# One hybrid layer on one core: the first block's memory, attention, state space and expert order rewritten

## The chip, the cores and the metric

The kernel runs on one core of one Trainium2 chip. A core has TensorE (PE: matmuls; its weight loads are shown as PEld), VectorE (DVE), ScalarE (ACT), GpSimd (POOL) and SyncE (SP), each with an instruction queue of its own that is worked off in order; they meet at semaphores. 16 DMA engines move data between HBM and the on-chip memory. The metric is device time of one launch in microseconds; the median of three runs is compared.

## The reference

Everything is fp32, one sequence of 256 rows of 1024. Two blocks follow each other; the change is in the first.

```
h = rms_norm(x, attn_norm_w)
z, xbc, dt, q, k, v, g_ssd, g_att = split(h @ w_in)            # 1024 x 7440
y_ssd = state_space(z, xbc, dt) @ w_ssd_out   # conv of 4, 16 heads of 64, 2 groups, chunks of 128; times silu(z); group norm
y_att = causal_attention(rope(q), rope(k), v) @ w_attn_out     # 16 heads of 64
x = x + (sigmoid(g_ssd) * y_ssd + sigmoid(g_att) * y_att) @ w_out
h = rms_norm(x, moe_norm_w)
x = x + moe(h)                  # 4 groups of 8 experts: one group, two experts a row; 1024 -> 256 -> 1024
x = x + sigmoid(rms_norm(x, ple_norm_w) @ w_ple_gate) * (p @ w_ple)
x = rms_norm(x, final_norm_w)
```

The second block (a long convolution beside a latent attention) takes this result. Its code changes only in a function's name and in where two vectors of norm weights are loaded and multiplied.

## The kernel before

**Products.** A fp32 product is made of three matmuls in a faster format (`mul3`): high part by high part, low by high and high by low. Weights come as tiles of 1 MB (four chunks of 128 rows by 512 columns) into four raw buffers; ACT makes the high part `WH` and DVE the low part `WL`, into three split slots. `weights(n)` splits every tile whose slot is free once tiles before n have been consumed; it stands at fixed places of the ACT and DVE queues. `gemm` multiplies two halves of 128 rows by a tile pair, 8 chunks of 6 matmuls. `transposed` turns a 256-row operand on TensorE into PSUM, and `high` and `low` split it on ACT and DVE.

**PSUM.** The 8 banks are handed out in turn by `ring.take(name, drainer)`, which makes TensorE wait until the drainer of the bank's last holder is done with it. `ring.of` narrows the set of banks.

**Order.** First norm, transposes; a transpose "colp" that turns row vectors (convolution weights and others) into columns; channel groups cx 0 to 2 (`channels`) with the convolution on ACT and DVE (`convolved`, L1759); q and k with rope on DVE (L1781 to L1789); v 0 and v 1; the state space's products cb and pv; transposes of q and k; attention head by head, with `fill` giving TensorE chunks of the z products between heads; the state space with chunks of the g products between its steps; the transposed attention output `oT`, the projections wao, wso, wo; the router `lg`; ranks; experts. Gates and z are drained by ACT with Sigmoid or Silu (`drain`, L1203).

**Experts.** Each row is copied into a slot of its experts (32 slots an expert). `gather` makes the slot inputs by matmuls with one-hot matrices; its stationary operands XNh and XNl are high and low parts of the normalized rows, written by ACT (L1374) and DVE (L2001). For q in 0 to 7, four experts are worked at a time: gate, up, down. Their 96 weight tiles, and one ("wpl") for a side product, are used unsplit, each in one of `NHELD` held buffers, which are carved out of memory that the first block no longer needs. Side products for rows that overflowed their slots' count are made near the end.

**SP's queue.** SP issues all weight DMAs in the order of use: `fetch(k)` (L2524) for dense tiles, which waits until the raw buffer's tile before was split, then `fetch_held(t)` (L2552) for expert tiles. A held buffer's first tile waits for the last reader of that memory, a later one for the last matmul of the tile before. `held_to` and `last_five` keep some buffers out of the rotation and say where the last five tiles go:

```python
held_to = {0: 0, 1: 0, 5: 0, 6: 0, 7: 0, 14: 56, 15: 56, 8: 68, 10: 85, 11: 85}
last_five = {92: 14, 93: 15, 94: 12, 95: 13, 96: 19}
...
for k in range(NRAW, dense_again):
    fetch(k)
for t in range(len(moe_tiles)):
    fetch_held(t)
```

## Time and profile before

| | |
|---|---|
| median of 3 runs | 888.27 us (887.16 to 888.43) |
| profiled execution | 888.41 us, span 886.6 us |
| mean granted TensorE clock | 0.942 of full speed |
| TensorE busy | 773.9 us, 87% |
| DVE, ACT, POOL busy | 472.9, 334.9, 17.8 us |
| DMA moved | 190.24 MB, 215 GB/s over the span |

The span is the time from the first to the last recorded instruction of one profiled execution; the metric has 1.8 us more around it. In the rows below times are microseconds from the span's start. A timeline's line is one instruction or several alike that follow each other (x16); "[5.30 <-DMA ...]" is the idle time of the engine before it and what ended it. In `pb<-HTh,WH` the operand that streams is named first and the stationary one second. Matmul durations overlap: the distance from one start to the next is what a matmul costs.

### The profile page before, as it was taken

The numbers are of one execution on the slowest core, as the hardware profiler recorded it, in microseconds if no ns is written. First come the engines' busy times: TensorE is split into PE (matmuls) and PEld (weight loads), VectorE is DVE, ScalarE is ACT, GpSimd is POOL, SyncE is SP. The second block draws the span as 40 slices with busy tenths as digits, with TensorE's granted clock in tenths as the row PEclk, the third lists the DMA queues.
The fourth block names the chain that finished last, engine by engine and source line by source line (L and its number), as shares of the span: only waits on it lengthen the run. The fifth ranks groups of instructions, "written<-read, shape, count | busy, mean of one in ns | idle before, by whom it ended". The sixth has DMA issues, their size and how long they took to land.

```text
span 886.6 us, 11023 instructions
## 1 busy us (share of the span) xinstructions
PE 773.9 (87%) x4618; PEld 578.0 (65%) x4618; DVE 472.9 (53%) x812; ACT 334.9 (38%) x487; POOL 17.8 (2%) x14
## 2 busy tenths in 40 slices
PE   2999798897998989797776988778999999999888
PEld 2988676676776877554442444335899965578676
DVE  4668946554666654722312411216777786754653
ACT  6454344543553422521100110105765534257512
POOL 0000000000000000000000000000010003000000
PEclk9999899898998999899888988988999999999989
DMA  8555541211442377989999999992455562433201
GB/s 268 196 185 194 190 136 55 95 48 52 142 139 95 97 273 320 422 318 407 420 422 421 421 421 420 421 390 75 152 191 173 166 237 95 143 110 124 99 1 48
DMA packets 62558, 190.24 MB, mean 215 GB/s; under 512 B 7405, under 2 KB 11751, under 8 KB 50024
## 3 DMA queue, kind: packets, MB, share of 16 engines
q1 hardware_dynamic: 60730, 184.70, 56.1%
q10 hardware_dynamic: 1774, 4.79, 1.7%
q8 instruction: 38, 0.62, 0.3%
q14 instruction: 16, 0.13, 0.0%
HBM read 188.42 MB, written 1.05 MB: 214 GB/s over the span
## 4 chain that ended last, share of the span: by engine, by line
PE 62%; DMA 16%; DVE 12%; ACT 7%; issue 2%; SPq 1%; POOL 0%; ACTq 0%; DVEq 0%
PE pb L498 59%; DMA raw<-in_w_exp_up 5%; DMA WHo<-in_w_exp_up 4%; DVE WL L1646 4%; ACT WH L1172 4%; DMA WLo<-in_w_exp_up 3%; PE pb L507 3%; DMA XN<-in_w_exp_up 3%; DMA arena<-in_final_norm_w 1%; DVE cv_ L1759 1%; ACT arena L1203 1%; SPq L2524 1%; SPq L2567 1%; DVE arenao L2001 0%; ACT arenao L1196 0%
## 5 line engine op out<-in xcount | busy, mean ns | idle before, releaser
L1646 DVE TENSOR_TENSOR WL<-raw,WH 128x2048 fp32r<-128x2048 f32 (+5 forms) x80 | 173.4, 2178 | 116.5 <-ACT WH L1172 116.5
L498 PE MATMUL pb<-WH,HTh 128*128 128x512 f32 (+2 forms) x416 | 171.6, 413 | 22.9 <-DVE HTl L1675 7.4
L1172 ACT ACTIVATE WH<-raw 128x2048 fp32r<-128x2048 f32 (+5 forms) x80 | 144.9, 1822 | 117.1 <-PE pb L498 113.3
L498 PE MATMUL pb<-WH,HTl 128*128 128x512 f32 (+2 forms) x416 | 163.4, 393 | 0.0
L498 PE MATMUL pb<-WL,HTh 128*128 128x512 f32 (+2 forms) x416 | 163.4, 393 | 0.0
L498 PEld LDWEIGHTS pb<-WH,HTh 128*128 128x128 f32 x416 | 80.5, 193 | 47.6 <-issue 7.3
L498 PEld LDWEIGHTS pb<-WL,HTh 128*128 128x128 f32 x416 | 80.2, 193 | 16.5
L498 PEld LDWEIGHTS pb<-WH,HTl 128*128 128x128 f32 x416 | 80.6, 194 | 14.8 <-issue 1.0
L498 PE MATMUL pb<-raw,arena 128*32 128x256 f32 x368 | 59.5, 507 | 18.8 <-DMA raw<-in_w_exp_up 9.1
L498 PE MATMUL pb<-arena 128*32 128x256 f32 (+6 forms) x284 | 71.3, 433 | 4.3 <-DMA arena<-in_w_exp_up 1.9
L2160 DVE TENSOR_TENSOR rt_<-rt_,pb 128x256 f32<-128x256 f32 x8 | 3.4, 422 | 109.1 <-ACT rt_ L1421 109.1
L498 PE MATMUL pb<-HTh,WH 128*128 128x256 f32 (+1 forms) x184 | 53.4, 290 | 0.0
L498 PE MATMUL pb<-HTh,WL 128*128 128x256 f32 (+1 forms) x184 | 53.0, 288 | 0.0
L498 PE MATMUL pb<-HTl,WH 128*128 128x256 f32 (+1 forms) x184 | 53.0, 288 | 0.0
L498 PEld LDWEIGHTS pb<-raw,arena 128*32 128x32 f32 x368 | 25.6, 143 | 40.6 <-issue 12.4
L498 PEld LDWEIGHTS pb<-arena 128*32 128x32 f32 (+4 forms) x284 | 34.3, 159 | 22.8 <-issue 9.3
L1421 ACT ACTIVATE rt_<-pb 128x256 f32<-128x256 f32 x8 | 3.1, 383 | 115.6 <-PE pb L498 115.6
L498 PE MATMUL pb<-WHo,arena 128*32 128x256 f32 (+1 forms) x160 | 38.3, 478 | 7.6 <-DMA WHo<-in_w_exp_up 5.6
L498 PE MATMUL pb<-XN,arena 128*128 128x64 f32 (+2 forms) x160 | 41.5, 414 | 2.8 <-DMA XN<-in_w_exp_up 1.8
L498 PE MATMUL pb<-WH,arenao 128*128 128x512 f32 x128 | 39.8, 392 | 0.0
L507 PE MATMUL pb<-c,arena 128*128 128x128 f32 (+2 forms) x202 | 29.2, 279 | 11.2 <-DMA arena<-in_final_norm_w 5.3
L507 PEld LDWEIGHTS pb<-c,arena 128*128 128x128 f32 (+2 forms) x202 | 24.5, 157 | 18.0 <-DMA arena<-in_final_norm_w 5.7
(357 smaller groups left out, 1308.6 us busy)
## 6 DMA issues: line engine op xcount, KB each, us to landing
raw<-in_w_in SPq DMA_DIRECT2D x46, 1024.0 KB, 5.1
raw<-in_w_exp_up SPq DMA_DIRECT2D x13, 1024.0 KB, 21.6
raw<-in_w_exp_gate SPq DMA_DIRECT2D x10, 1024.0 KB, 23.7
WLo<-in_w_exp_down SPq DMA_DIRECT2D x10, 1024.0 KB, 19.6
raw<-in_w_out SPq DMA_DIRECT2D x8, 1024.0 KB, 5.4
WHo<-in_w_exp_down SPq DMA_DIRECT2D x8, 1024.0 KB, 19.4
raw<-in_w_attn_out SPq DMA_DIRECT2D x6, 1024.0 KB, 5.5
arena<-in_w_exp_up SPq DMA_DIRECT2D x5, 1024.0 KB, 11.8
```

The lines of the kernel that those rows point to most:

```text
L498: return e.matmul(o, l, r, start=start, stop=stop, skip_group_check=True)
L507: return e.transpose(o, i, ident[0:k, 0:k])
L1172: e.activation(h_, r_, ACT.Copy).then_inc(hi.sem, hi.mark(k))
L1203: e.activation(dst[:, t, :], pb((name, t))[:, 0:n], f, scale=scale).then_inc(ac.sem, ac.mark((name, t)))
L1421: e.activation(HG[q % 2], pb(("gu", q))[:, 0:256], ACT.Silu).then_inc(ac.sem, ac.mark(("su", q)))
L1646: e.tensor_tensor(l_, r_, h_.bitcast(F32), ALU.subtract).then_inc(lo.sem, lo.mark(k))
L1759: e.scalar_tensor_tensor(out=cv[:, s:L], in0=u[:, 0:L - s], scalar=cw[:, 3 - s, g:g + 1], in1=cv[:, s:L], op0=ALU.mult, op1=ALU.add).then_inc(
L2160: e.tensor_tensor(HG[q % 2], HG[q % 2], pb(("gu", q))[:, 256:512], ALU.mult).then_inc(ve.sem, ve.mark(("gu", q)))
L2524: e.dma_start(dst[:, :, col:col + v.shape[2]], v).then_inc(d.sem, d.mark(k, by=16))
L2567: e.dma_start(dst, src).then_inc(d_rows.sem, d_rows.mark("in", by=16))
```

## The change

- *Start:* DVE scales both halves of the first norm (before, ACT scaled one), the first tile is split ahead of it, and "colp" is turned after the first channel group.
- *Rope and v:* the tile that falls due is split before the rope except for the last one; v 0 takes the banks of the xs transposes; q's and k's transposes stand between v 0 and v 1.
- *Attention:* two heads a step in two banks, 11 steps with two chunks of z or g each; mask and maximum in one DVE operation; eight score buffers instead of four.
- *z and g:* drained by plain copies; Silu of z's left half and the Sigmoids of g run later on ACT from memory.
- *State space:* by groups of 8 heads, the product of a group one step behind its decay rows; the attention output's transposes and splits stand between the steps, into buffers of their own (OT).
- *Transposes by halves:* mT inside wso 1 and wo 0, nm inside wo 1 and the router (`halves_T`). Rows of w_out and the routers are taken in "(c p)" order.
- *Gather:* XNh and XNl are contiguous rows in HT's memory, and the gather's stationary operand has a step of 8 elements.
- *Experts:* 19 held buffers instead of 20, in another order, x no longer among them. SP issues expert tiles 0 to 5 between dense tiles and 6 and 7 right behind them on conditions of that stage; two routers' DMAs stand behind dense tile 7.

```diff
-NHELD = 20
+NHELD = 19
...
+        OT = tuple(arena_r[:, o:o + 2048].rearrange("p (c l) -> p c l", c=8) for o in (6656, 0))
...
+        XNh, XNl = (x.rearrange("p c l -> p (c l)").rearrange("p (t d) -> p t d", t=2) for x in HT)
...
+        XG = [x.rearrange("p (c e) -> p c e", c=8) for x in (X.rearrange("p t d -> p (t d)"), arena[:, 6144:8192])]
...
+        for key, w, rows_ in (("wao", wao, "(p c)"), ("wso", wso, "(p c)"), ("wo", wo, "(c p)")):
...
+        held = [part(16896), part(12800), part(2048), part(4096), XN.rearrange("p t d -> p (t d)"), part(10752), part(8704),
+                part(14848), *last_raw, *[x[:, s, :] for s in emptied for x in (WHf, WLf)], part(0)]
...
+        held_to = {0: 0, 1: 0, 5: 0, 7: 0, 16: 56, 17: 56, 6: 68, 3: 80, 12: 85, 13: 85, 4: 76}
+        last_five = {92: 16, 93: 17, 94: 14, 95: 15, 96: 4}
...
             rows_T("n1")
+            channels(("cx", 0), [("xbc", g) for g in range(4)], 512, "n1", [ve] * 4)
             d_rows.wait_ge(e, "in")
-            turn(ring.take("colp", ve)[:, 0:122], rows[0:122, :]).then_inc(mm.sem, mm.mark("colp"))
-            channels(("cx", 0), [("xbc", g) for g in range(4)], 512, "n1", [ve] * 4)
+            turn(ring.take("colp", ve)[:, 0:114], rows[0:114, :]).then_inc(mm.sem, mm.mark("colp"))
             channels(("cx", 1), [("xbc", g) for g in range(4, 8)], 512, "n1", [ve] * 4)
             channels(("cx", 2), [("xbc", 8), ("xbc", 9), "dtT"], 272, "n1", [ve, ve, ac])
...
+            gemm(("v", 0), ("v", 0), HT, "n1", (ve, ac), [where[("xs", t, 0)] for t in range(2)])
...
+            gemm(("v", 1), ("v", 1), HT, "n1", (ve, ac))
...
+            def scores(j):
+                o = [ring.take(("s", h), ve) for h in (2 * j, 2 * j + 1)]
                 for n in ("qT", "kT"):
                     ve.wait_ge(e, (n, 4))
                     ac.wait_ge(e, (n, 6))
-                mul(o[:, 0:128], QT[of:of + 64, j, 0:128], KT[of:of + 64, j, 0:128])
-                mul(o[:, 128:384], QT[of:of + 64, j, 128:256], KT[of:of + 64, j, 0:256]).then_inc(
-                    mm.sem, mm.mark(("s", h)))
+                for t in range(2):
+                    w = 128 * (t + 1)
+                    for i, of in enumerate((0, 64)):
+                        ins = mul(o[i][:, 128 * t:128 * t + w], QT[of:of + 64, j, t * 128:t * 128 + 128],
+                                  KT[of:of + 64, j, 0:w])
+                        if t:
+                            ins.then_inc(mm.sem, mm.mark(("s", 2 * j + i)))
...
+            for j in range(11):
+                if j < 8:
+                    scores(j)
+                fill(1)
+                if 2 <= j <= 9:
+                    weights_T(2 * j - 4)
+                    weights_T(2 * j - 3)
+                fill(1)
+                if j >= 3:
+                    values(2 * j - 6)
+                    values(2 * j - 5)
...
+            def attended_T(js):
+                for j in js:
+                    o = ring.take(("oT", "T", j), ve)
+                    ve.wait_ge(e, ("o", 1, 0), ("o", 1, 1))
+                    for c in (j, j + 1):
+                        for t in range(2):
+                            o_ = (c - j) * 256 + t * 128
+                            ins = turn(o[:, o_:o_ + 128], O[:, t, slice(c, c + 127 * 8 + 1, 8)])
+                    ins.then_inc(mm.sem, mm.mark(("oT", "T", j)))
+
+            def states(t, g):
+                o = ring.take(("y", t, g), ve)
+                ve.wait_ge(e, ("km", t, g))
+                for h in range(8 * g, 8 * g + 8):
+                    ins = mul(o[:, (h - 8 * g) * 64:(h - 8 * g) * 64 + 64], LM[:, h, :], XD[:, t, h * 64:h * 64 + 64])
+                ins.then_inc(mm.sem, mm.mark(("y", t, g)))
+                if t == 1:
+                    o = ring.take(("yi", g), ve)
+                    ve.wait_ge(e, ("pv", 0))
+                    ac.wait_ge(e, ("pv", 1))
+                    mul(o[:, :], XBC[g * 64:g * 64 + 64, 9, 128:256], PV[g * 64:g * 64 + 64, :]).then_inc(
+                        mm.sem, mm.mark(("yi", g)))
...
+            def halves_T(name, src, half, ready):
+                ve.wait_ge(e, ready)
+                for j in (4 * half, 4 * half + 2):
+                    o = ring.take((name, "T", j), ve)
+                    for c in (j, j + 1):
+                        for t in range(2):
+                            o_ = (c - j) * 256 + t * 128
+                            ins = turn(o[:, o_:o_ + 128], src[:, t, c * 128:c * 128 + 128])
+                    ins.then_inc(mm.sem, mm.mark((name, "T", j)))
...
+            for k in range(5):
+                if k < 4:
+                    decay_rows(k // 2, 8 * (k % 2))
...
+                    decay_rows(k // 2, 8 * (k % 2) + 4)
+                    fill(2)
+                if k in (1, 2):
+                    attended_T((4 * k - 4, 4 * k - 2))
+                if k:
+                    states((k - 1) // 2, (k - 1) % 2)
+                    fill(2)
...
-            gemm(("wao", 0), ("wao", 0), HT, "oT", (ve, ve))
+            gemm(("wao", 0), ("wao", 0), OT, "oT", (ve, ve))
             ve.wait_ge(e, "yn")
             transposed("yT", lambda t: XN[:, t, :], 8)
-            gemm(("wao", 1), ("wao", 1), HT, "oT", (ve, ve))
-            for i in range(2):
-                gemm(("wso", i), ("wso", i), YT, "yT", (ve, ve))
-            ve.wait_ge(e, ("mg", 1))
-            transposed("mT", lambda t: MG[:, t, :], 8)
...
+            def gemm_around(key, lhs, ready, at, between):
+                o = [ring.take((key, t), ve) for t in range(2)]
+                for c in range(8):
+                    gemm_chunk(key, key, c, o, lhs, ready)
+                    if c == at:
+                        between()
+
+            gemm_around(("wso", 1), HT, "yT", 4, lambda: halves_T("mT", MG, 0, ("mg", 0)))
+            gemm_around(("wo", 0), OT, "mT", 2, lambda: halves_T("mT", MG, 1, ("mg", 1)))
+            gemm_around(("wo", 1), OT, "mT", 4, lambda: halves_T("nm", X, 0, ("x mix", 0)))
+
...
+            for half in range(2):
+                for c in range(4 * half, 4 * half + 4):
+                    ve.wait_ge(e, ("nm", c))
+                    ins = mul3(o[0:36, 0:256], tuple(x[:, c, :] for x in WR), tuple(x[:, c, :] for x in HT), c == 0,
+                               c == 7)
+                if half == 0:
+                    halves_T("nm", X, 1, ("x mix", 1))
...
-                            ins = mul(o[:, (c % 2) * 256:(c % 2) * 256 + 256], x[:, t, c, :],
+                            ins = mul(o[:, (c % 2) * 256:(c % 2) * 256 + 256], x[:, t, slice(c, c + 127 * 8 + 1, 8)],
...
+                if name == ("z", 0):
+                    drain(name, Z[:, :, 0:512], ACT.Copy)
+                elif name == ("z", 1):
+                    ac.wait_ge(e, (("z", 0), 1))
+                    e.activation(Z[:, :, 0:512], Z[:, :, 0:512], ACT.Silu).then_inc(ac.sem, ac.mark("z left"))
+                    drain(name, Z[:, :, 512:1024], ACT.Silu)
...
+                    mm.wait_ge(e, ("s", 15))
+                    drain(name, (GS, GA)[i // 2][:, :, 512 * (i % 2):512 * (i % 2) + 512], ACT.Copy)
...
+            weights(None, 1)
...
+            for i in (2, 3, 0, 1):
+                gv = (GS, GA)[i // 2][:, :, 512 * (i % 2):512 * (i % 2) + 512]
+                ac.wait_ge(e, (("g", i), 1))
+                e.activation(gv, gv, ACT.Sigmoid).then_inc(ac.sem, ac.mark(("gate 1", i)))
...
+                for t in range(2):
+                    e.tensor_scalar(XN[:, t, :], src[:, t, :], norm_of[n][:, t:t + 1], None, ALU.mult).then_inc(
+                        ve.sem, ve.mark(("xn", n)))
...
+            mm.wait_ge(e, "colp")
+            e.tensor_copy(colp, pb("colp")[:, 0:114]).then_inc(ve.sem, ve.mark("colp"))
...
+                weights(used((n, i)) - 1)
...
+                for t, cut in enumerate((slice(0, 128), slice(128, 384))):
+                    ins = e.tensor_tensor_reduce(S1[s][:, cut], pb(("s", h))[:, cut], C["matt"][:, cut], -0.125, 3.0e38,
+                                                 ALU.add, ALU.min, nmx[:, s, t:t + 1])
+                ins.then_inc(ve.sem, ve.mark(("s", h), ("mx", h)))
...
-                e.scalar_tensor_tensor(out=XNl[:, t, :, :], in0=Xc[:, t, :, :], scalar=rnm[:, t:t + 1],
-                                       in1=XNh[:, t, :, :].bitcast(F32), op0=ALU.mult, op1=ALU.subtract).then_inc(
+                e.scalar_tensor_tensor(out=XNl[:, t, :], in0=X[:, t, :], scalar=rnm[:, t:t + 1],
+                                       in1=XNh[:, t, :].bitcast(F32), op0=ALU.mult, op1=ALU.subtract).then_inc(
...
+                elif i == 2:
+                    mm.wait_ge(e, ("yi", 1), ("oT", "T", 6))
+                elif i == 3:
+                    ve.wait_ge(e, "yn")
+                elif i == 4:
+                    mm.wait_ge(e, ("yT", "T", 6))
+                elif i == 5:
                     ve.wait_ge(e, (("wao", 1), 1))
+                elif i == 6:
+                    ve.wait_ge(e, ("mg", 1))
+                elif i == 7:
+                    mm.wait_ge(e, ("mT", "T", 6))
                 elif i in held_raw:
...
+            early = {used_before(("wso", 0), 4): (0, 1, 2), used_before(("wso", 1), 4): (3, 4),
+                     used_before(("wo", 0), 4): (5,)}
+            for k in range(8, dense_again):
+                fetch(k)
+                for t in early.get(k, ()):
+                    fetch_held(t)
+            for t in range(6, len(moe_tiles)):
                 fetch_held(t)
```

## Rows read from the trace of the kernel before

**Rows 1.** The page, busy time of the engines over the span.

```profile
PE 773.9 (87%) x4618; PEld 578.0 (65%) x4618; DVE 472.9 (53%) x812; ACT 334.9 (38%) x487; POOL 17.8 (2%) x14
```

**Rows 2.** Busy time by stretch; columns: stretch, length, engines' busy time (instructions), clock, DMA share, GB/s.

```profile
98.43:138.73 40.30, 32.65 (x164) 26.51 (x163) 26.09 (x33) 16.68 (x20) 0.00 (x0) 0.92 0.49 156
206.86:278.78 71.92, 64.69 (x341) 53.62 (x342) 44.14 (x65) 36.29 (x39) 0.00 (x0) 0.97 0.38 123
278.78:354.06 75.28, 72.24 (x320) 59.36 (x320) 39.45 (x48) 22.01 (x21) 1.01 (x1) 0.96 0.55 202
393.43:587.10 193.67, 157.06 (x1343) 79.14 (x1336) 46.94 (x113) 20.63 (x38) 0.00 (x0) 0.89 1.01 415
```

**Rows 3.** SP's timeline; columns: start, length, queue, line, operation, target<-source, count.

```profile
321.48 2.66 SPq L2552 DMA_DIRECT2D arena<-in_w_exp_gate  x2
...
371.08 0.33 SPq L2552 DMA_DIRECT2D X<-in_w_exp_up  x1
382.26 3.78 SPq L2552 DMA_DIRECT2D raw<-in_w_exp_down  x3
393.43 0.33 SPq L2552 DMA_DIRECT2D arena<-in_w_exp_down  x1
...
572.58 0.33 SPq L2552 DMA_DIRECT2D X<-in_w_exp_down  x1
```

**Rows 4.** TensorE's timeline, stalls before the first expert; in brackets idle time before and releaser.

```profile
19.34 0.47 PE L507 MATMUL pb<-c,arena 122*128 122x122 f32 x1 [5.30 <-DMA arena<-in_final_norm_w]
...
106.35 0.77 PE L498 MATMUL pb<-WH,HTh 128*128 128x512 f32 x1 [5.33 <-DVE rt_ L1784]
...
135.11 2.84 PE L507 MATMUL pb<-c,arena 128*128 128x128 f32 x24 [1.55 <-DVE arena L1685]
...
204.25 2.82 PE L498 MATMUL pb<-arena,rt_ 128*128 128x64 f32 x12 [5.76 <-DVE rt_ L1685]
...
278.78 0.77 PE L498 MATMUL pb<-WH,HTh 128*128 128x512 f32 x1 [3.88 <-DVE HTl L1675]
...
329.76 2.06 PE L507 MATMUL pb<-c,arena 128*128 128x128 f32 x16 [2.84 <-DVE arena L1974]
...
371.09 6.37 PE L498 MATMUL pb<-cv_o,arenao 128*128 128x256 f32 x32 [4.36 <-DVE arenao L2001]
```

**Rows 5.** ScalarE's timeline, a high part near the start.

```profile
33.64 1.79 ACT L1172 ACTIVATE WH<-raw 128x1904 fp32r<-128x1904 f32 x1 [3.28 <-PE pb L498]
```

**Rows 6.** VectorE's timeline, the operations used as prices.

```profile
37.52 1.90 DVE L1759 SCALAR_TENSOR_TENSOR cv_<-pb,small,cv_ 128x255 f32<-128x255 f32 x4
...
100.63 2.29 DVE L1646 TENSOR_TENSOR WL<-raw,WH 128x2048 fp32r<-128x2048 f32 x1 [0.95 <-ACT WH L1172]
...
268.60 1.22 DVE L1915 TENSOR_TENSOR arena<-arena,cv_ 128x1024 f32<-128x1024 f32 x1
...
365.89 2.05 DVE L2001 SCALAR_TENSOR_TENSOR arenao<-X,small,arenao 128x1024 fp32r<-128x1024 f32 x1
```

**Rows 7.** TensorE's timeline, the product cb and one head's step.

```profile
130.06 0.72 PE L498 MATMUL pb<-arena 64*128 64x128 f32 x8
...
176.00 0.92 PE L498 MATMUL pb<-arena 64*128 64x128 f32 x4
176.85 0.50 PE L498 MATMUL pb<-WH,HTh 128*128 128x512 f32 x1
...
178.34 0.49 PE L507 MATMUL pb<-c,arena 128*128 128x128 f32 x3
...
179.38 0.48 PE L498 MATMUL pb<-arena 64*128 64x128 f32 x2
```

**Rows 8.** TensorE's timeline, transposes whose stationary operand has a step of 8.

```profile
272.86 2.05 PE L507 MATMUL pb<-c,arena 128*128 128x128 f32 x16
```

**Rows 9.** TensorE's timeline, the side products and the last "down".

```profile
585.22 7.03 PE L498 MATMUL pb<-XN,arena 128*128 128x512 f32 x16
596.72 1.06 PE L498 MATMUL pb<-WLo,rt_ 128*32 128x512 f32 x1 [4.48 <-issue]
```

More of the change, by code:

```diff
@@ new lines, in scalar @@
+            for j in range(11):
+                if j < 8:
+                    exps1(2 * j)
+                    exps1(2 * j + 1)
+                fill(1)
+                if 2 <= j <= 9:
+                    h = 2 * j - 3
+                    if h >= 4:
+                        mm.wait_ge(e, ("pv1", h - 4))
+                    drain_t(("p", h), P1[:, h % 4, 0:384])
+                fill(1)
+            for k in range(5):
+                if k < 4:
+                    for h0 in (8 * (k % 2), 8 * (k % 2) + 4):
+                        ve.wait_ge(e, ("lm", k // 2, h0))
+                        e.activation(LM[:, h0:h0 + 4, :], LM[:, h0:h0 + 4, :], ACT.Exp).then_inc(
+                            ac.sem, ac.mark(("lm", k // 2, h0)))
+                        fill(2)
+                if k in (1, 2):
+                    high("oT", OT, 4 * k, after=("pv1", 15), first=4 * k - 4)
+                if k:
@@ new lines, in vector, with decay_rows @@
+                fill(1)
+                if j in (6, 10):
+                    divided(2 * j - 5)
+            def decay_rows(t, h0):
+                mm.wait_ge(e, ("lm", t, h0))
+                if t:
+                    mm.wait_ge(e, ("y", 0, h0 // 8))
+                for h in range(h0, h0 + 4):
+                    ins = e.scalar_tensor_tensor(
+                        out=LM[:, h, :], in0=pb(("lm", t, h0))[:, (h - h0) * 128:(h - h0) * 128 + 128],
+                        scalar=Ac[:, t, h:h + 1], in1=C["mneg"], op0=ALU.subtract, op1=ALU.add)
+                ins.then_inc(ve.sem, ve.mark(("lm", t, h0)))
@@ new lines, in vector @@
+            mm.wait_ge(e, ("p", 15))
+            for k in range(5):
+                if k < 4:
+                    for h0 in (8 * (k % 2), 8 * (k % 2) + 4):
+                        decay_rows(k // 2, h0)
+                        fill(2)
+                    skipped(k // 2, k % 2)
+                if k in (1, 2):
+                    low("oT", OT, 4 * k, first=4 * k - 4)
+                if k:
+                    states((k - 1) // 2, (k - 1) % 2)
+                if k < 4:
+                    t, g = k // 2, k % 2
@@ L1986, in residual @@
                         ve.sem, ve.mark((name, t), event))
-            for i in range(2):
-                residual(("wo", i), i, ("x mix", i))
-                weights(used(("wo", i)))
+            residual(("wo", 0), 0, ("x mix", 0))
+            weights(used(("wo", 0)))
+            low("nm", HT, 4, mnc)
+            residual(("wo", 1), 1, ("x mix", 1))
             ve.wait_ge(e, ("x mix", 1))
```

384 lines of the change are left out of this document (144 added, 240 removed).

## The prediction

> **What bounds the kernel now.** I read the page first, then busy time by stage, then SP's queue, then TensorE's timeline for its stalls and the other engines' beside them. The page shows TensorE busy 87% of the span [rows 1]: a gain must come out of its idle stretches or its work, wherever TensorE sets the pace. The windows show where it does not. From 393.4 to 587.1 the DMA share is 1.01 at 415 GB/s while TensorE works 157 of 193.7 us [rows 2]; 415 GB/s is 2.5 us for each tile of 1 MB. So the expert phase is bound by the transfer, with 36.6 us of slack on TensorE. Everything before it, and everything behind it, goes by TensorE.
>
> What links the two is SP's queue [rows 3]. Expert tiles start at 321.48, and after 382.26 SP issues three and then nothing until 393.43, when the first "down" releases a buffer; from there the queue runs full. The transfer-bound stretch therefore begins when TensorE reaches the first "down". A microsecond saved before it moves the whole stretch one microsecond. The early issue itself fetches tiles that are due anyway before that point: at 393.43 all the held tiles are in, and no buffer is free for another. Counting tiles by the order of releases, 23 are fetched or under way at the first "down" in either version and 74 remain, with 19 buffers as with 20. I cost the early issue and the smaller ring at nothing. The cover is the stretch in which SP waits (382.26 to 393.43); without it each tile by which the queue starts richer would be worth 2.5 us.
>
> The sum is made against the profiled execution, 888.4 us (span 886.6), 0.1 above the median shown, 888.27. About 0.2% (1.8 us) is what a measurement of this kernel can tell from no change.
>
> **A, the start.** TensorE waits 5.30 us for the DMA of the row vectors before the "colp" transpose at 19.34 [rows 4]. That transpose moves behind the first channel group, so the group starts 4.9 earlier. But banks are taken round-robin: "colp" no longer takes the bank after the first transposes, so the fourth bank of the second channel group is now the one that xbc 0 holds, which DVE frees only at the end of `convolved(0)`. In front of that stand ACT's two high parts and first tap (1.8 for a high part [rows 5]) and DVE's two low parts and three scalar-tensor steps (2.3 each, and 0.5 each from four in 1.90 [rows 6]), in order: from about 26.8, when ACT gets to them by my count, to about 34.6. TensorE, done with group 0 near 27.6, idles about 7, starts group 1 at 34.6 against 32.2 before, and loses about 2 more to a lowered clock, as after the 5.33 stall at 106.35, where a matmul took 0.77 against 0.50 at full clock [rows 4, 7]. A 0.8 stall behind it goes away. Cost +1.9; bounds −4.9 (no bank wait) to +2.7.
>
> **B, rope to scores** (98.43, where k1 ends, to 138.73, where the first scores start: 40.3 us [rows 2]). Before, v0 waits 5.33 for rope's last read of its bank at 106.35 [rows 4]. After, rope's tile is split before the rope and v0 takes the xs banks, so what is late is the split behind the WL at 100.63 [rows 6]: v0 starts near 101.7, 3.3 after k1. Then 11 for v0, 32 transposes at 0.12 (24 took 2.84 at 135.11 [rows 4]) with 1 us of waits, 4.5 together, 11 for v1, and 5.5 until scores (a high and low part, a copy of v, a copy of cb), against 8.7 before. 35.3: −5.0. Bounds: TensorE's whole idle time of the stage, 7.65 [rows 2], gone; or only the one at v0 shortened, −1.
>
> **C, attention** (138.73 to 206.86, 68.1 us, with 16 z chunks). A head's step took 3.38: scores 0.85, a chunk 1.49 (178.34 less 176.85), and 1.04 for three transposes and the six matmuls of the values, of which I give the transposes 0.33 and the values 0.71 [rows 7]. Two heads at rows 0 to 63 and 64 to 127, into two banks, may run side by side: the eight 64-row matmuls of cb alternate halves and took 0.72 in all, less than the 0.92 of one head's four [rows 7]. I take 0.95 for a pair (bounds 0.85 to 1.7). A pair's step is then 0.95 + 2 × 1.4 + 0.66 + 1.42 + 0.16 of seams = 5.99 against 6.76. Eight of these and six chunks more at 1.4 are 56.3, 0.4 for the first exponentials, 1.3 for banks that wait behind the Silu of z: 58.0. So −10.1, though six g chunks (8.3 us) are already in it. The stall of 5.76 at 204.25 [rows 4], TensorE waiting for the last heads' copies with nothing to fill, is filled by them. The mask and maximum in one DVE pass replace four DVE operations; nothing like it is in the trace (from one 0.56 add to the add and two reductions), and DVE is off the path here, so 0. Bounds −14 to −4 (pairs not concurrent: 8 × 0.75 more).
>
> **D, state space** (206.86 to 278.78, 71.9 us [rows 2]). Six g chunks fewer: −8.3. TensorE idles 7.23 there [rows 2]: 3.88 at the end, waiting for the transposed attention's low part at 278.78 [rows 4], and 3.35 inside, before chunks whose bank ACT drains with a table to load. The drains are plain copies now and the transposes and splits are done inside: −7.2. New: the first decay bank is held by the division of heads 8 to 15 (+1.9), the last group's product (+0.7), and wao's bank behind the last g drain (+1.2). −11.7. Bounds −15.5 to −6.
>
> **E, output projections** (278.78 to 354.06, 75.3 us [rows 2]). wao 0 took 13.5 instead of 11 because its clock had fallen (the stage's first matmul takes 0.77 and not 0.50 [rows 4, 7]); the 2.84 wait for mT at 329.76 [rows 4] and its transposes are put between chunks by halves. New: four sigmoids on ACT after g stand before the state space's norm, near 12.4 us after g 3 with table load, squares and scaling, of which 0.3 shows behind wao 0's 11. 66 for six projections, 0.3, 1.75 for yT, 2.7 for halves: 71.0, −4.3. Bounds −5 to −2.
>
> **F, routing to the first "down"** (354.06 to 393.43). Half of nm's transposes move into wo 1: −1.9. Two low parts of the gather on DVE, 2.05 each through a strided view [rows 6], become contiguous; 1.22 is the row for as many contiguous elements [rows 6]: −1.7. ACT's highs shrink too; DVE waits for the first of them alone, and I add nothing. −3.6; bounds −6 (the gather's 32 matmuls at 371.09 took 6.37 after a stall of 4.36, at the lower clock [rows 4]) to 0. **A rule that speaks against this.** The contiguous halves are now read with a step of 8 elements, 32 bytes, as the gather's stationary operand. The Trainium skill, SBUF — State Buffer, section Door 1: The DMA port swizzle, says that a 16-byte line must be hit twice to hide its latency, and that fp32 can be strided by up to 4 elements for free. By it DVE gains here, as the two rows show, and the gather's weight loads lose; it gives no price, and the sum by it is rival 3's. The trace has 16 transposes with such a stationary operand in 2.05 [rows 8], 0.13 each, against 0.12 of the contiguous ones at 135.11 [rows 4]: by these the sum stays, and I add nothing.
>
> **H, the tail.** Buffers for the last tiles change. Before, the last expert tile is issued at 572.58 [rows 3] and waits for nothing on TensorE's side. After, tile 95 takes the buffer of the overflow weights, so SP can issue it only when the 16 side products at 585.22 are done, 592.3 [rows 9]. It and the last tile behind it land some 5 and 7.7 us later, at 600.0, against the last "down" at 596.72 [rows 9]: +3.3, bounds 0 to +5.
>
> Sum: +1.9 − 5.0 − 10.1 − 11.7 − 4.3 − 3.6 + 3.3 = −29.5; small new waits that I can't place, +1.5. −28.0: **860.4 us**. Its own range is 851 to 868.
>
> **Rivals.**
> 1. *In-order queues eat half of C and D* (0.17). DVE is busy 44.1 of D's 71.9 [rows 2]; with the transposed attention's low parts (2.5) and without the splits of six g chunks (3.4) it must fit 43 into 60; the queue is in order, so an early decay step waits behind a fill's split. For it: stalls like 204.25 and 278.78 were all on DVE [rows 4]. Against: 0.72 busy fits. Half of 21.8 lost gives 871 (868 to 880).
> 2. *Less stands in the way than I charge* (0.13). No bank wait at the start (−6.8 against A), the gather at full clock (−2.4), no extra waits (−1.5): 849.7; with the tail also free 846. If instead the queue did start richer by eight tiles, 20 us less: 840; SP's idle stretch [rows 3] speaks against it.
> 3. *The strided gather* (slower, 0.06). 128 matmuls read the strided halves: 48 before the first "down", the other 80 inside the phase with 36.6 us of slack [rows 2]. To undo 28 it must cost (28 + 36.6)/128 = 0.50 us a matmul more, from there on the time is above 888, at 0.6 about 901. The strided transposes' 0.01 [rows 8] speaks against it.
> 4. *The gains don't carry* (0.04): something else, such as the last held tile's arrival, sets the first "down", and the phase starts at its old time: 888 ± 1.8. SP's rows show the last of the first tiles issued at 371.08 and the first release only at 382; after the change they are issued earlier still.
>
> **How the numbers follow.** My forecast, 0.60: 851 to 868. With the shares above, 846 leaves out about 0.06 of rival 2, and 877 about 0.03 of rival 1 and all of rivals 3 and 4: the range 846 to 877 leaves out a little under 0.2. Faster 0.90, same 0.04, slower 0.06.
>
> **What would show it.** After: TensorE's first channel group near 14.6, then an idle 7 ended by DVE's convolution (A); no stall before v0 over 4 (B); pairs of scores near 0.95 and a pair's step near 6 (C); the first output projection near 254, at full clock (D, E); the first "down" near 361, and from it tiles every 2.5 us until the last but two; SP's tile behind the side product, and the last "down" 3 later than the side products' end gives (H); the last 285 us as long as before. Wrong if the first "down" moves and the end doesn't, if scores of a pair take 1.7, or if the gather's matmuls are slower than 0.3.

## The result, and the profile after

The changed kernel takes 874.6 us (median of 4 runs, 871.98 to 877.03) against 888.35 before in the same comparison: 0.9845 of the time (95% interval 0.9814 to 0.9876), 13.8 us less. A second set of 5 runs gave 873.84 and again 0.9845 (0.9826 to 0.9865). The forecast was 28.0 less, 860.4. The sign was right and 874.6 lies in the wide range (846 to 877), but it is outside the forecast's own range (851 to 868), and the gain is 13.8 of the 28.0 that were forecast, a little under half. The profiled execution took 874.9 us, span 873.1, 13.5 less than before.

The page of the changed kernel, busy times (answers to [rows 1]):

```profile
PE 771.7 (88%) x4618; PEld 580.5 (66%) x4618; DVE 459.9 (53%) x813; ACT 326.1 (37%) x483; POOL 17.8 (2%) x14
```

TensorE is busy 2 us less than before, DVE and ACT 13 and 9 us less. Of the 13.5 us that the span lost, 11.3 are idle time of TensorE, as the forecast wanted it; there is less of it than forecast.

Busy time by stretch of the changed kernel, columns as in [rows 2]: rope and v, attention, state space, output projections, routing to the first "down", expert phase. The fifth ends where the first "down" frees a buffer and SP issues the next tile (372.22 below); TensorE starts that "down" at 368.02.

```profile
101.05:135.33 34.28, 30.88 (x164) 25.08 (x163) 24.97 (x33) 17.00 (x20) 0.00 (x0) 1.00 0.54 181
135.33:201.28 65.95, 58.77 (x340) 47.45 (x340) 28.81 (x87) 32.93 (x84) 0.00 (x0) 0.92 0.27 86
201.28:261.30 60.02, 57.06 (x305) 47.46 (x305) 39.47 (x62) 22.43 (x27) 0.00 (x0) 0.97 0.33 103
261.30:331.62 70.32, 70.24 (x329) 58.29 (x329) 41.75 (x49) 31.87 (x35) 1.01 (x1) 1.00 0.78 306
331.62:372.22 40.60, 33.90 (x275) 23.61 (x277) 18.49 (x71) 11.44 (x23) 0.70 (x1) 0.87 0.64 253
372.22:560.34 188.12, 153.28 (x1288) 81.82 (x1284) 45.27 (x107) 20.27 (x37) 0.00 (x0) 0.91 1.00 406
```

These stretches end at the same events as the terms B to F of the sum, and the last one where the 94th of the 97 tiles lands. (That landing, 560.34 here and 579.61 before, is read from the trace's DMA records; SP issued it at 543.15 below.) So term stands against measurement:

| term | before | after | change | forecast |
|---|---|---|---|---|
| A, start to the end of k1 | 98.43 | 101.05 | +2.6 | +1.9 |
| B, to the first scores | 40.30 | 34.28 | −6.0 | −5.0 |
| C, attention | 68.13 | 65.95 | −2.2 | −10.1 |
| D, state space | 71.92 | 60.02 | −11.9 | −11.7 |
| E, output projections | 75.28 | 70.32 | −5.0 | −4.3 |
| F, to the first "down" | 39.37 | 40.60 | +1.2 | −3.6 |
| expert phase, to the 94th tile | 186.18 | 188.12 | +1.9 | 0 |
| the rest (tail H, second block) | 307.00 | 312.76 | +5.8 | +3.3 |
| small waits, not placed | | | | +1.5 |
| sum | | | −13.5 | −28.0 |

A, B, D and E are right within 1.0 each. C is 7.9 off, F 4.8, the two last stretches 4.4. How far one execution can be trusted shows in a second trace of the changed kernel, from the second set of runs: C 67.09, F 41.75 and the expert phase 186.64 instead of 65.95, 40.60 and 188.12, A 0.6 longer, B, D and E within 0.03.

TensorE's timeline of the changed kernel, its stalls and one pair of scores (answers to [rows 4] and [rows 7]):

```profile
14.97 0.35 PE L497 MATMUL pb<-HTh,WH 128*128 128x256 f32 x1 [0.72 <-DVE HTl L1727]
...
34.34 0.58 PE L497 MATMUL pb<-HTh,WH 128*128 128x256 f32 x1 [7.52 <-DVE cv_ L1806]
...
104.29 0.47 PE L497 MATMUL pb<-WH,HTh 128*128 128x512 f32 x1 [0.65 <-ACT arena L1234]
...
135.33 0.93 PE L497 MATMUL pb<-arena 64*128 64x128 f32 x8 [2.75 <-DVE cv_ L1900]
...
152.68 0.87 PE L506 MATMUL pb<-c,arena 128*128 128x128 f32 x6 [1.16 <-DVE rt_ L1733]
...
156.15 0.93 PE L497 MATMUL pb<-arena 64*128 64x128 f32 x8
...
183.79 0.77 PE L497 MATMUL pb<-WH,HTh 128*128 128x512 f32 x1 [4.41 <-ACT arena L1230]
...
201.28 1.62 PE L497 MATMUL pb<-c,small 128*128 128x128 f32 x8 [1.62 <-DVE arena L1931]
```

The first channel group starts at 14.97 and the 7.52 us idle behind it, ended by DVE's convolution, is what term A foresaw (14.6 and about 7). The 5.33 before v0 is 0.65. The eight score matmuls of two heads take 0.85 (156.15 to 157.00), as much as four of one head did before, and less than the 0.95 that was taken. But there are four stalls inside the attention and at its end (2.75, 1.16, 4.41, 1.62), for which the sum has 1.7 in C and 1.9 in D; the first of them (at 135.33) lies in B's last 5.5, as forecast, and behind it the granted clock falls to the lower level in this execution.

ScalarE's timeline of the changed kernel ahead of the 4.41:

```profile
180.37 1.28 ACT L1246 ACT_TABLE_LOAD   x1
181.66 1.06 ACT L1246 ACTIVATE arena<-arena 128x1024 f32<-128x1024 f32 x1
182.62 1.07 ACT L1230 ACTIVATE arena<-pb 128x512 f32<-128x512 f32 x2
```

ACT loads a table, takes the Silu of z's left half out of memory, and only then drains z's second half with Silu; 183.69 is when the second of these drains ends, and 0.1 later TensorE goes on. The chunks that fill the steps have two banks of their own, and g's first chunk needs them. (Of z only the left half is drained by a plain copy.) The exponentials ahead of the table load start late as well. ACT's first of them, and DVE's timeline before it:

```profile
178.12 0.40 ACT L1356 ACTIVATE arena<-arena,small 128x128 f32<-128x128 f32 x1 [4.74 <-DVE small L1920]
```

```profile
173.03 2.29 DVE L1693 TENSOR_TENSOR WL<-raw,WH 128x2048 fp32r<-128x2048 f32 x1 [3.18 <-ACT WH L1202]
...
177.45 0.28 DVE L1920 CUSTOM_DVE_ANT_0 arena<-pb,c 128x128 f32<-128x128 f32 x1
```

TensorE had finished this pair's scores at 174.32. DVE worked off a low part (2.29), a copy and the division of heads 0 to 7 first and began their mask and maximum (L1920) at 177.45; ACT stood idle for 4.74 until then.

### The profile page after: what moved, and what is told of

The parts are those of the page before. It is cut to its first block, busy times and chain, and to the rows that moved or that the text cites. A ratio compares the mean times of both kernels' runs of the same rounds, so it can differ in the third digit from the quotient of the medians.

```text
span 873.1 us, 11016 instructions
## 1 busy us (share of the span) xinstructions
PE 771.7 (88%) x4618; PEld 580.5 (66%) x4618; DVE 459.9 (53%) x813; ACT 326.1 (37%) x483; POOL 17.8 (2%) x14
## 4 chain that ended last, share of the span: by engine, by line
PE 60%; DMA 17%; DVE 12%; ACT 8%; issue 2%; POOL 0%; SPq 0%; ACTq 0%; DVEq 0%
PE pb L497 57%; DMA raw<-in_w_exp_up 7%; DVE WL L1693 5%; DMA WHo<-in_w_exp_up 5%; ACT WH L1202 4%; PE pb L506 3%; DMA WLo<-in_w_exp_up 3%; DMA raw<-in_w_in 1%; DMA XN<-in_w_exp_down 1%; DVE cv_ L1806 1%; ACT arena L1230 1%; ACT arena L1356 1%; DVE HTl L1727 0%; ACT arena L1388 0%; POOL small L2572 0%
## 5 line engine op out<-in xcount | busy, mean ns | idle before, releaser
L497 PE MATMUL pb<-WH,HTh 128*128 128x512 f32 (+2 forms) x384 | 158.4, 413 | 16.5 <-ACT arena L1230 5.4
L497 PE MATMUL pb<-WH,HTl 128*128 128x512 f32 (+2 forms) x384 | 150.1, 391 | 0.0
L497 PE MATMUL pb<-WL,HTh 128*128 128x512 f32 (+2 forms) x384 | 150.0, 391 | 0.0
L497 PE MATMUL pb<-arena 128*32 128x256 f32 (+6 forms) x252 | 59.0, 444 | 3.2 <-DVE cv_ L1900 2.8
L497 PE MATMUL pb<-WH,arenao 128*128 128x512 f32 x192 | 59.9, 393 | 1.2 <-ACT arena L1230 1.2
L497 PE MATMUL pb<-raw,arena 128*32 128x256 f32 x224 | 37.4, 520 | 10.3 <-DMA raw<-in_w_exp_gate 6.2
L497 PEld LDWEIGHTS pb<-WH,arenao 128*128 128x128 f32 x192 | 35.6, 188 | 8.9 <-ACT arena L1230 1.6
L497 PEld LDWEIGHTS pb<-HTh,WH 128*128 128x128 f32 (+1 forms) x184 | 35.2, 191 | 9.2 <-DVE cv_ L1806 7.7
L497 PE MATMUL pb<-WL,arenao 128*128 128x512 f32 x96 | 37.4, 390 | 0.0
L497 PEld LDWEIGHTS pb<-HTh,WL 128*128 128x128 f32 (+1 forms) x184 | 35.3, 192 | 0.2
```

What stands on the lines that cost most here:

```text
L497: return e.matmul(o, l, r, start=start, stop=stop, skip_group_check=True)
```

## The experiments

Each run is the changed kernel with the edit shown; its ratio is to the kernel before, and the changed kernel's is 0.9845 (0.9814 to 0.9876). "Less" compares medians with the changed kernel's 874.6.

### The last tiles' buffers (H)

```diff
-        last_five = {92: 16, 93: 17, 94: 14, 95: 15, 96: 4}
+        last_five = {84: 18, 85: 15, 91: 12, 92: 16, 93: 17, 94: 14, 95: 15, 96: 4}
...
+            if t in last_five and i in ring:
+                ring.remove(i)
```

> The changed kernel, with other buffers for the last expert tiles: the fourth and third of the last five now go where a tile of the seventh quarter lay, and the side product's weights move to a buffer that no last tile needs. Theory: in the changed kernel two of the last tiles wait at SP for TensorE (issued at 564.40 and 574.16 after the tile before them at 543.15) and so the last one lands at 583.01 and the last down starts its last products at 583.06. With the buffers free earlier all are issued by about 550 and land by about 568, and the last down starts when the side products and the branch behind them are over, near 577 to 578.5: 4.5 to 6 us less, about 869 to 870. Rival: the side products and the norm weights behind them set the end anyway, less than 1.5 us.

869.72 us, 0.9787 (0.9768 to 0.9805): 4.9 less. SP's and TensorE's timelines, first the changed kernel:

```profile
332.66 26.18 SPq L2624 DMA_DIRECT2D arena<-in_w_exp_up  x2
358.88 0.43 SPq L2624 DMA_DIRECT2D arena<-in_w_exp_down  x1
...
372.22 0.33 SPq L2624 DMA_DIRECT2D raw<-in_w_exp_down  x1
...
543.15 0.43 SPq L2624 DMA_DIRECT2D WLo<-in_w_exp_down  x1
564.40 0.33 SPq L2624 DMA_DIRECT2D WHo<-in_w_exp_down  x1
574.16 0.33 SPq L2624 DMA_DIRECT2D WLo<-in_w_exp_down  x1
```

```profile
567.10 7.03 PE L497 MATMUL pb<-WLo,arena 128*128 128x512 f32 x16
575.64 0.62 PE L497 MATMUL pb<-WLo,rt_ 128*32 128x512 f32 x1 [1.51 <-issue]
...
579.23 1.92 PE L497 MATMUL pb<-WLo,rt_ 128*32 128x512 f32 x2 [2.54 <-DMA WLo<-in_w_exp_down]
583.06 1.06 PE L497 MATMUL pb<-XN,rt_ 128*32 128x512 f32 x1 [1.91 <-DMA XN<-in_w_exp_down]
```

and with the edit:

```profile
542.95 0.43 SPq L2626 DMA_DIRECT2D WLo<-in_w_exp_down  x1
543.42 0.43 SPq L2626 DMA_DIRECT2D WHo<-in_w_exp_down  x1
552.69 0.33 SPq L2626 DMA_DIRECT2D WLo<-in_w_exp_down  x1
```

```profile
567.79 7.03 PE L499 MATMUL pb<-arena 128*128 128x512 f32 x16
579.24 1.06 PE L499 MATMUL pb<-WLo,rt_ 128*32 128x512 f32 x1 [4.42 <-issue]
```

The waits at SP (564.40 for a buffer that the "up" of the last four experts reads, 574.16 for the side products, which take 567.10 to 574.1) are gone, and the last "down" starts whole at 579.24 where its last tile's products started at 583.06. The mechanism of H is shown; its size was 4.9 by the medians and not 3.3. One thing is left open: between the side products and the last "down" TensorE stands 1.51 in the changed kernel and 4.42 with the edit, as before the change [rows 9], at the same branch.

### The bank at the start (A), and whether the start carries

```diff
+            colp_bank = ring.take("colp", ve)
             channels(("cx", 0), [("xbc", g) for g in range(4)], 512, "n1", [ve] * 4)
...
-            turn(ring.take("colp", ve)[:, 0:114], rows[0:114, :])
+            turn(colp_bank[:, 0:114], rows[0:114, :])
```

> The changed kernel, with the bank of the row vectors' transpose taken ahead of the first channel group (the transpose itself stays behind it). The second group's fourth bank is then that one again and not the one that the first convolution holds. Theory: the idle 7.52 us at 34.34 goes away, and about 1.5 of lowered clock behind it; the next waits give back 0 to 2. First down 6.5 to 9 us earlier, and the whole as much: 866 to 868. Rival: the split of the next tiles and the convolutions in VectorE's queue take its place, 3 us or less gained. Second rival: the start moves by 7 but the end does not, because the expert phase is not released by TensorE's first down.

865.27 us, 0.9744 (0.9723 to 0.9766): 9.3 less, 0.7 below the range that was expected. The second group's start, and the first scores:

```profile
27.58 0.38 PE L497 MATMUL pb<-HTh,WH 128*128 128x256 f32 x1 [0.37 <-DVE small L1798]
...
126.95 0.92 PE L497 MATMUL pb<-arena 64*128 64x128 f32 x7 [2.75 <-DVE cv_ L1901]
```

The 7.52 is 0.37. First scores at 126.95 instead of 135.33, the first "down" at 360.78 instead of 368.02, the span 863.7 instead of 873.1. What is saved at the start arrives at the end, through the transfer-bound phase, as the forecast had it: an earlier TensorE frees the buffers earlier that SP's queue waits for.

### The Silu of z (C)

```diff
-                    ac.wait_ge(e, (("z", 0), 1))
-                    e.activation(Z[:, :, 0:512], Z[:, :, 0:512], ACT.Silu)...
-                    drain(name, Z[:, :, 512:1024], ACT.Silu)
+                    drain(name, Z[:, :, 512:1024], ACT.Copy)
...
+            for i in range(2):      # after the attention's steps
+                zv = Z[:, :, 512 * i:512 * i + 512]
+                e.activation(zv, zv, ACT.Silu)...
```

> The changed kernel, with the second half of z drained by a plain copy too and both Silus done between the attention and the state space. Theory: TensorE's stall of 4.41 us at 183.79 is the wait for the two fixed banks of the filling products, and 2.3 of it are the table load and the Silu of the left half that ScalarE does before it drains; it falls to about 2, and part of the 1.9 us of lowered clock behind it goes too: 2.3 to 4 us less, 870.5 to 872.5. Rival: the stall comes from VectorE, whose mask and maximum stand behind a split and hold back ScalarE's exponentials; less than 1 us gained.

869.63 us, 0.9788 (0.9748 to 0.9829): 5.0 less by the medians, where 2.3 to 4 were expected, but the interval overlaps the changed kernel's. The attention takes 62.84 in the profile. With its code unchanged it took 63.9 to 67.1 in six traces, whose stalls are the same within 0.03; what differs is the time at the lower clock behind them. So the stall itself is the measure here:

```profile
181.01 0.77 PE L497 MATMUL pb<-WH,HTh 128*128 128x512 f32 x1 [2.02 <-ACT arena L1230]
```

The stall falls from 4.41 (4.40 or 4.41 in all six traces) to 2.02, by the 2.3 that stood on ACT in front of the drain. The rest is the wait for one pair of banks, which ACT drains behind the exponentials of its step; and those start late, as shown above, because DVE's mask and maximum stand behind a low part and a division. That part is read from the trace; no run moved the work on DVE there.

### The g products out of the attention (C)

The lists of work to fill with get g behind the attention's loop instead of ahead of it, in all three queues.

> The changed kernel, with the g products kept out of the attention (the attention's steps are filled by z alone, as before the change; the state space gets all 32 chunks of g). Theory: what the six chunks of g in the attention save by covering the last heads (a stall of 5.8 before the change) they lose again, since the first of them waits 4.41 us for the two fixed banks of the filling products and runs 1.9 slower behind that: within 2 us of the changed kernel, 872.5 to 876.5. Rival: the cover is worth the full 5 to 6 us, 879 to 881.

876.29 us, 0.9866 (0.9841 to 0.9891), 1.7 more than the changed kernel and within what can't be told from it.

```profile
187.30 5.38 PE L497 MATMUL pb<-arena,rt_ 128*128 128x64 f32 x24 [6.35 <-DVE rt_ L1733]
194.30 1.01 PE L497 MATMUL pb<-c,small 128*128 128x128 f32 x3 [1.62 <-DVE arena L1929]
```

The end of the attention now stalls 6.35 with nothing to fill, as it did before the change (5.76, [rows 4]); and the stall of 4.41 is not there. Attention and state space take 127.6 us together, against 126.0 (123.6 to 127.1 in the six traces with the attention of the changed kernel). So the cover that C counted on is real, a stall of 6.35, and the bank's wait behind z took most of it back.

### The gather's operands (F)

XNh and XNl are laid out as before the change: `"p (t c j) -> p t c j"`, written through a strided view of x, read by TensorE as `x[:, t, c, :]`.

> The changed kernel, with the gather's two operands laid out as before the change: written through a strided view by ScalarE and VectorE, read by TensorE contiguously. Theory: the step of 8 elements costs each gather matmul about 0.05 us at the lower clock and 0.10 at the full one; 32 in 7.88 us go back to about 6.3 and 16 in 4.15 to about 2.2, 3.5 us less before the first down, while the low parts go from 1.28 back to 2.05 each, 1.5 more: net 1 to 2.5 us less, 872 to 873.5. Rival: the lower clock explains the slower gather; its matmuls stay at 0.24 and the time rises by 1.5.

871.87 us, 0.982 (0.9791 to 0.9848): 2.7 less, though the interval overlaps the changed kernel's; the size is read from the traces. TensorE's weight loads for the gather by shape (busy us, mean ns), of the kernel before, the changed kernel and this one, and one low part on DVE of the last two:

```profile
L498 PEld LDWEIGHTS pb<-cv_o,arenao 128*128 128x128 f32 x128 | 18.1, 218 | 5.1 <-DVE arenao L2001 4.4 <-DVE sg_o L2166 0.7
```

```profile
L497 PEld LDWEIGHTS pb<-cv_o,HTl 128*128 128x128 f32 x64 | 21.6, 338 | 0.0
```

```profile
342.08 1.28 DVE L2070 SCALAR_TENSOR_TENSOR HTl<-X,small,HTh 128x1024 fp32r<-128x1024 f32 x1
```

```profile
L498 PEld LDWEIGHTS pb<-cv_o,HTl 128*128 128x128 f32 x64 | 13.6, 213 | 0.0
```

```profile
341.44 2.05 DVE L2071 SCALAR_TENSOR_TENSOR HTl<-X,small,HTh 128x1024 fp32r<-128x1024 f32 x1
```

Windows over a gather of 32 and one of 16 matmuls, columns as in [rows 2] (the granted clock is the third from the end), of the changed kernel and of this one:

```profile
345.75:353.63 7.88, 7.88 (x32) 7.75 (x32) 2.91 (x14) 1.42 (x3) 0.00 (x0) 0.60 0.01 2
411.17:415.20 4.03, 4.03 (x19) 3.90 (x17) 0.91 (x2) 0.47 (x1) 0.00 (x0) 1.00 1.01 421
```

```profile
346.65:352.56 5.91, 5.91 (x33) 5.78 (x34) 2.77 (x14) 1.42 (x3) 0.00 (x0) 0.63 0.00 0
362.79:364.90 2.11, 2.11 (x17) 1.98 (x17) 0.62 (x2) 0.47 (x1) 0.00 (x0) 1.00 1.04 423
```

With the step of 8 a load takes 338 ns instead of 213 to 218 (means over both clock levels), and each matmul 0.25 (32 in 7.88, 16 in 4.0 to 4.15) instead of 0.13 at full clock (16 in 2.11) and 0.19 at a granted clock of 0.63 (32 in 5.91).

The strided gather has a second price, in the clock. These are the gate and up products behind the first gather, in the second trace of the changed kernel and in this run:

```profile
356.53:367.30 10.77, 10.02 (x137) 5.71 (x137) 2.31 (x11) 1.11 (x2) 0.00 (x0) 0.84 0.41 149
```

```profile
353.71:362.79 9.08, 8.33 (x137) 5.07 (x137) 2.31 (x11) 1.11 (x2) 0.00 (x0) 1.00 0.47 184
```

In all seven traces with the strided gather the granted clock falls to its lower level (1.2 GHz) at least once more between the first gather and the end of the first "down": in six in these products (10.6 to 10.8 us instead of 9.08), in the first trace of the changed kernel in the second gather, at a granted clock of 0.72. In none of the six traces with a contiguous gather does it fall there. Why it does is not shown.

From the gather's start to the first "down" the changed kernel needs 22.27 us (23.8 to 24.0 in the other six traces), this one 18.25 (18.2 to 18.6 in the other five); it gives 1.6 back between router and gather, where DVE's low parts take 2.05 again instead of 1.28. The rule of the Trainium skill that was weighed (SBUF — State Buffer, section Door 1: The DMA port swizzle) has the sign right on both sides of the change, writer and reader. The trace's own row that was set against it, transposes with the same step at 0.13 [rows 8], did not carry over to the gather; why those loads don't pay is not shown by any run here.

### Early expert tiles

`early = {}`, and all held tiles fetched behind the dense ones.

> The changed kernel, with no expert tile issued between dense tiles: the first six too are issued behind the last dense tile. Theory: the issue of tiles ends at a full ring long before the first release (all 19 are issued by 332.7 and the next waits until 358.9), so 15 us of transfer more behind the dense tiles still end by about 360 and the first down does not move: within 1.5 us of the changed kernel's 874.6. Rival: each early tile is worth its 2.5 us, so 10 to 15 us more, 885 to 890.

872.19 us, 0.9807 (0.9778 to 0.9835): 2.4 less where at most 1.5 either way was expected, and the intervals of the two overlap. Tiles issued early are worth nothing that can be told, as the forecast had it. The changed kernel's SP rows above say why: the 19 buffers are full at 332.66, and the next tile waits 26 us for a release.

### Together

The edits of the last tiles, the bank, the Silu and the gather:

> The changed kernel with four edits together: the last tiles' buffers, the bank of the row vectors, the Silus of z after the attention, the gather's operands contiguous. Theory: the three on the way to the first down add up, since each takes idle time or work out of TensorE's stream ahead of it, and the fourth lies behind: by the single runs 4.9 + 9.3 + 5.0 + 2.7, up to 21.9 us less, 852.7, and 855 if the medians of single runs flatter some of them. Rival: one stall hides another, or the transfers of the expert tiles, which start earlier against the dense tiles, become the limit: less than 14 us together, above 860.

856.32 us, 0.9633 (0.9596 to 0.9671): 18.3 less than the changed kernel, where the single runs add up to 21.9 and 855 was the upper end of what was expected. And with `ring.of, ring.i = range(6), 0` ahead of the state space:

> The four edits together, and the bank counter set back to the first bank ahead of the state space, so that the first decay rows do not wait for the bank that the division of heads 8 to 15 holds. Theory: the stall of 1.62 us there and up to 1.5 of lowered clock behind it go: 1 to 3 us less than with the four edits. Rival: VectorE works the division off before the decay rows anyway, so the wait moves to the next bank: within 0.5.

851.06 us, 0.9577 (0.9555 to 0.9599). The first decay rows start without a stall:

```profile
188.87 1.11 PE L500 MATMUL pb<-c,small 128*128 128x128 f32 x8
```

Against the profile of the four edits the attention with the wait at its end takes 59.7 us instead of 61.5, the state space 57.0 instead of 60.0, the output projections 71.6 instead of 70.3: 3.4 less in all. The medians differ by 5.3, more than the 1 to 3 expected; the traces bear out 3.4 of it.

The start of the expert phase now looks different. SP's timeline:

```profile
347.86 0.43 SPq L2632 DMA_DIRECT2D arena<-in_w_exp_down  x1
...
355.19 0.33 SPq L2632 DMA_DIRECT2D raw<-in_w_exp_down  x1
```

The first gate and up products free four buffers, and SP issues the 20th to the 23rd tile into them, the last of these here at 347.86; the first "down" frees the next at 355.19. By the trace's DMA records the 23rd tile lands at 358.42, 3.2 us after that. In the kernel before it landed at 392.04, 1.4 ahead of the first release by "down" (393.43), in the changed kernel at 371.40, 0.8 ahead of it (372.22). So here the transfer is behind already when the first "down" ends, and the phase takes 189.3 us from there, 3.1 more than before the change. In all six traces in which the 23rd tile lands late the phase takes 188.3 to 189.7, in five of the seven in which it lands ahead 185.6 to 186.6 (in the other two 188.1 and 189.2). What TensorE gains between the first gate products and the first "down" then no longer arrives at the end in full; no run set out to show it. Two more versions:

> The five edits together (last tiles' buffers, bank of the row vectors, Silus after the attention, contiguous gather, bank counter), and no expert tile issued between dense tiles. Theory: with the first down now near 351 the ring of 19 is still full before it needs the tiles, since 19 tiles issued from about 300 land in 47 us, but only just: 0 to 2 us difference to the version with early tiles. Rival: the early tiles compete with dense tiles on the way to the first down and cost time: 2 us or more faster without them. Third: the stages ahead have become so short that the late tiles hold up the first quarters: 3 us or more slower.

850.22 us, 0.9583 (0.9561 to 0.9605): no difference, so the early tiles are still worth nothing that can be told, with the first "down" 17 us further ahead.

> The five edits together, and in VectorE's queue the copy of the transposed weights of the even head ahead of the split that the filling product brings due. Theory: the stall of 1.1 us at the third pair (TensorE waits for this copy, which stands behind a 2.29 us low part) goes, and the later pairs gain nothing since they had no stall: 1 to 1.5 us less than with the five edits. Rival: the copy waits for TensorE, so the split behind it is late and the next chunk of z waits for it: 0 to 2 us more.

851.3 us, 0.9603 (0.9583 to 0.9623): no difference. The 1.1 us stall behind the split is gone, but two of 0.3 stand in its place, and the wait for the pair of banks is 1.64 where it was 2.02; the attention takes 60.2 instead of 59.7:

```profile
147.32 0.47 PE L500 MATMUL pb<-WH,HTh 128*128 128x512 f32 x1 [0.31 <-ACT arena L1234]
...
152.60 0.93 PE L500 MATMUL pb<-arena 64*128 64x128 f32 x8 [0.32 <-DVE small L1928]
...
171.62 0.77 PE L500 MATMUL pb<-WH,HTh 128*128 128x512 f32 x1 [1.64 <-ACT arena L1234]
```

The version with five edits is 37 us ahead of the kernel before and 23 of the changed one; none shown is faster beyond its interval, for the last two can't be told from it.

> The changed kernel itself once more, on the chip and beside the runs of the versions below, so that they have a common base. Both theories: 0.982 to 0.987 of the kernel before, as it was.

873.84 us, as told above.

## Why the prediction was right in sign and wrong in size

**What bounds it.** Right. The expert phase stayed bound by the transfer (DMA share 1.00, TensorE 153 of 188 us), its start moved with TensorE, and early tiles changed nothing that can be told. The start's 8.4 us, when they were taken away, came through (7.2 at the first "down", 9.4 at the span's end). That the phase begins with the first "down" holds in the changed kernel by 0.8 us only: in six of the runs' traces the last of the four tiles that the first gate and up products release lands only after it. No run varied the ring's size, so its cost of nothing is not shown; in the changed kernel the transfer stands still while the ring is full (DMA share 0.01 from 345.75 to 353.63, above).

**A, B, D, E.** Right, each within 1.0, A's idle 7 us at its place and with its cause. The forecast charged A as a cost; the bank edit shows that nothing else stood there. Two sums are not clean: the parts that A names make 2.4 + 2 − 0.8 = 3.6 and not 1.9 (measured 2.6), and E's add up to 70.75 and not 71.0 (measured 70.32). And D is right in part by where a wait fell: the 1.9 for the first decay bank was charged to D, but its 1.62 lie in front of the decay rows and so at C's end. C and D together were to give 21.8 and gave 14.1.

**C failed**, in the term "1.3 for banks that wait behind the Silu of z". It measured 4.41 idle and, at the lower clock behind it, 2.0 more for what TensorE does up to 189.35 (a chunk at 183.79 in 2.69 and not 1.49, six transposes in 1.13 and not 0.57, the next chunk 0.25 more): 6.4. Of the 4.41, 2.3 are the table load and the left half's Silu, as an edit shows; the other 2.0, by the trace, are exponentials that wait for DVE. Of what else C lost, 1.2 is the copy behind a split at 152.68, about 1.6 the lower clock behind the stall at 135.33, and 1.6 the wait of the decay rows. The parts at the lower clock are of this execution; they differ from one to the next, as above. The pair's step itself was cheaper than forecast, 5.77 and not 5.99, 1.8 in eight.

**F failed** in "by these the sum stays, and I add nothing". The strided loads cost 32 × 0.05 and 16 × 0.12, 3.5 us, before the first "down", and the clock fell once more: 0.5 of it shows in the first "down" itself, and in the other traces 1.6 in the gate products. Ahead of the gather 2.9 of the 3.6 came. Rival 3 named the mechanism, with a break-even of 0.50 a matmul; it measured 0.05 to 0.12, enough to take F's gain and not enough to decide.

**H** was right in mechanism and mis-sized: 4.9 by the edit against 3.3. The largest part of the difference is in the traces: the last tile was to land 7.7 us after the side products freed a buffer and landed 8.9 after (574.16 to 583.01).

**Rivals.** The time is the one of rival 1 (868 to 880), which came nearer than the forecast in its cause too: queues in order took part of C. On DVE, the queue that it names, the traces show 1.2 at 152.68, the 2.0 at 183.79 and 1.6 at 201.28; it lacked the table load and Silu in ACT's queue (2.3), and the gather. Rival 2's premise, that less stands in the way, was wrong throughout. Rival 4 is refuted by the bank edit. The 1.9 us that the expert phase took longer can't be put down to the change: in the second trace of the same kernel it is 0.5, with F 1.2 longer there.

## What to carry to other kernels

When work is moved to fill a stall, look for what the moved work itself must own: here the fill had one pair of banks, and its drain stood behind a function that needed a table and behind exponentials that waited for another engine. An analogue for a price must share the instruction's role: a strided transpose did not price a strided gather. And a counter that hands out banks makes every earlier edit move the owner of every later bank; two stalls here (7.5 and 1.6 us) were such owners, and an edit of a line or two removed each.

## What the runs showed of the hardware

A 128 x 128 weight load with a step of 32 bytes took 338 ns, and its matmuls stood 0.25 us apart at either clock (0.246 in a stretch with a granted clock of 0.60, 0.25 at full clock), where contiguous ones stood 0.19 apart at a granted clock of 0.63 and 0.13 at full clock. Transposes with the same step hardly paid (0.13 each, against 0.12). Two heads' score matmuls on rows 0 to 63 and 64 to 127, into two banks, took no longer than one head's (0.85 for eight and for four). One DVE pass that adds a mask and keeps the extreme took 0.28 us for 128 and 0.42 us for 256 columns; the next head's began 0.55 after them, where before the add alone took 0.56 a head and two reductions (0.29 and 0.41) and a scaling (0.17) followed it.
